# Who negates the weights: moving a per-piece negation from ScalarE to the queue that loads them

## The reference, cut to what matters

```
for l in range(2):                       # first kind
    h = rms_norm(x, norm1) * (1 + sc1) + sh1
    x = x + g1 * hybrid_mixer(h, w_in, w_out, ...)
    h = rms_norm(x, norm2) * (1 + sc2) + sh2
    x = x + g2 * conv_ffn(h, w_gate, w_val, conv_w, conv_b, w_down)
x = rms_norm(x, final_norm)
for l in range(2):                       # second kind
    h = rmsnorm(x, norm_mix_pre); proj = h @ w_in
    y_att = sliding_window_attention(...) @ w_o_att
    y_rw  = rwkv7_time_mix(...) @ w_o_rw
    x = x + rmsnorm((sigmoid(gate_a) * y_att + sigmoid(gate_b) * y_rw) @ w_out, norm_mix_post)
    x = x + rmsnorm((gelu(ua) * ub) @ w_down, norm_ffn_post)     # ua, ub = conv(rmsnorm(x) @ w_up)
    x = x + rmsnorm(sigmoid(x @ w_ple_gate) * (p @ w_ple), norm_ple)
```

## Time and profile before

| | |
|---|---|
| median of 3 runs | 4455.27 us (4441.81 to 4456.62) |
| the profiled execution, its own time | 4447.68 us |
| its span, first to last instruction | 4445.8 us |
| mean granted clock | 0.956 |
| PE busy | 3942.4 us, 89% of the span |
| VectorE, ScalarE, GpSimd busy | 2143.0, 1723.3 and 791.4 us |

### The profile page before, as it was taken

The page is one execution under the profiler, slowest core; times in us unless marked ns, Lnnn a source line. Parts: engine busy times, 40 slices in busy tenths (PEclk is TensorE's granted clock), DMA queues, the critical chain, the costliest instruction groups (busy, mean ns, idle before and its releaser), DMA issues.

```text
span 4445.8 us, 70148 instructions
## 1 busy us (share of the span) xinstructions
PE 3942.4 (89%) x29148; PEld 3156.2 (71%) x29148; DVE 2143.0 (48%) x3621; ACT 1723.3 (39%) x2512; POOL 791.4 (18%) x1108
## 2 busy tenths in 40 slices
PE   5987999898799978899999799967889999979996
PEld 4675778776588856777777588855667777758884
DVE  5674651147333146266663466125536666346603
ACT  3364222346333246344443322234534444332223
POOL 1111222211222211200001222211120000222221
PEclk9998999999899989999999899988999999989998
DMA  9844998874488853732226589954373222658894
GB/s 279 237 101 107 283 270 186 186 157 94 104 187 188 188 121 80 169 67 53 63 59 134 119 189 188 192 123 111 86 163 72 52 53 53 149 119 187 187 192 108
DMA packets 189741, 628.75 MB, mean 141 GB/s; under 512 B 22768, under 2 KB 27888, under 8 KB 189040
## 3 DMA queue, kind: packets, MB, share of 16 engines
q0 software_dynamic: 158976, 549.52, 57.2%
q1 hardware_dynamic: 24048, 65.28, 4.1%
q10 hardware_dynamic: 6400, 9.44, 0.8%
HBM read 612.63 MB, written 2.10 MB: 138 GB/s over the span
## 4 chain that ended last, share of the span: by engine, by line
PE 43%; DVE 9%; ACT 6%; DMA 3%; issue 2%; ACTq 0%; POOL 0%; DVEq 0%; SPq 0%
PE bank L214 10%; PE bank L215 10%; PE bank L216 10%; PE bank L1922 5%; PE bank L1885 1%; ACT L2078 1%; ACT at_s L1505 1%; ACT w_lo L154 1%; ACT w L2078 1%; PE bank L1983 1%; PE bank L1911 1%; PE bank L1981 1%; DVE rw_z L2340 1%; ACT gate L2078 1%; DVE at_s L1696 1%
## 5 line engine op out<-in xcount | busy, mean ns | idle before, releaser
L214 PE MATMUL bank<-h_hi,w_hi 128*128 128x512 f32 x2576 | 1067.0, 414 | 90.1 <-DMA w_lo<-in_b_wq 33.3
L215 PE MATMUL bank<-h_lo,w_hi 128*128 128x512 f32 x2576 | 1025.2, 398 | 0.0
L216 PE MATMUL bank<-h_hi,w_lo 128*128 128x512 f32 x2576 | 1023.9, 397 | 0.0
L154 ACT ACTIVATE w_lo<-w_hi 128x1024 fp32r<-128x1024 f32 (+2 forms) x552 | 556.0, 1011 | 1175.0 <-DMA w_hi<-in_a_wgv 326.2
L214 PEld LDWEIGHTS bank<-h_hi,w_hi 128*128 128x128 f32 x2576 | 489.3, 190 | 240.8 <-issue 118.0
L215 PEld LDWEIGHTS bank<-h_lo,w_hi 128*128 128x128 f32 x2576 | 489.2, 190 | 118.1 <-issue 10.8
L216 PEld LDWEIGHTS bank<-h_hi,w_lo 128*128 128x128 f32 x2576 | 487.9, 189 | 119.4
L2078 ACT ACTIVATE gate<-bank 128x512 f32<-128x512 f32 x80 | 47.8, 597 | 274.6 <-PE bank L1922 274.6
L1365 DVE TENSOR_SCALAR fa_conv<-fa_a_in,par_a 128x512 f32<-128x512 f32 x44 | 21.6, 492 | 242.2 <-ACT fa_a_in L1312 242.0
L214 PE MATMUL bank<-fa_y_hi,w_hi 128*128 128x512 f32 x352 | 137.3, 390 | 1.2 <-DMA w_lo<-in_a_wd 1.2
L214 PE MATMUL bank<-fb_y_hi,w_hi 128*128 128x512 f32 x352 | 137.1, 389 | 0.1
(11 more groups left out here) (468 smaller groups left out, 7842.7 us busy)
## 6 DMA issues: line engine op xcount, KB each, us to landing
w_hi<-in_a_wgv POOLq DMA_DIRECT2D x80, 512.0 KB, 5.4
w_lo<-in_a_wgv POOLq DMA_DIRECT2D x80, 512.0 KB, 7.7
w_hi<-in_b_wup POOLq DMA_DIRECT2D x80, 512.0 KB, 5.2
w_lo<-in_b_wup POOLq DMA_DIRECT2D x80, 512.0 KB, 7.4
w_hi<-in_a_wh POOLq DMA_DIRECT2D x48, 512.0 KB, 4.7
w_lo<-in_a_wh POOLq DMA_DIRECT2D x48, 512.0 KB, 5.7
fa_ada_raw<-in_ada SPq DMA_DIRECT2D x48, 512.0 KB, 7.4
w_hi<-in_b_wrkv POOLq DMA_DIRECT2D x48, 512.0 KB, 4.3
```

The lines of the kernel that those rows point to most:

```text
L154: st.do(st.eng.activation(self.lo[:, s], self.hi[:, s].bitcast(F32), ACT.Copy, scale=-1.0), (self.neg_made, n + 1))
L214: pe.matmul(out, self.hi[:, a], hh[:, k0 + k, :], start=first and k == 0, stop=False)
L215: pe.matmul(out, self.hi[:, a], hl[:, k0 + k, :], start=False, stop=False)
L216: mm = pe.matmul(out, self.lo[:, a], hh[:, k0 + k, :], start=False, stop=last and k == ks - 1)
```

## The change

Seven edits, made together:

1. GpSimd negates (`tensor_scalar`, one SBUF input) between the load and the adding load of a piece; all of ScalarE's calls of `ws.high` and `first_pieces` are gone.
2. The one-column Ln that brings the table in becomes `act_ready`; at most edges it stands ahead of the wait for the last product instead of behind the last square.
3. At the edges out of ma, fa, mx and fb, VectorE adds square m-1 to the sum before it handles product m, not behind it.
4. The row swaps of attention are issued on SyncE's queue, each behind ScalarE's copy.
5. In RWKV the variance product, its Ln and its Exp come ahead of the pair's k projection and first exponentials; a one-column Ln stands ahead of the copy of r.
6. In RWKV's VectorE program `rt` is formed behind `at`, the bonus product is read three chain steps later or more, the end-of-chunk factors (`bbar`) are made earlier, the product r*k*r_k is written to `kp` instead of `r`.
7. Two PSUM banks change places (2 and 3), and the waits that guard them with them.

The diff, cut to what the prediction speaks of:

```diff
+    def negate(self, pool, n):
+        s = self.span(n)
+        pool.wait_ge(self.hi_in[n % self.FLAGS], self.landed(n))
+        pool.tensor_scalar(self.lo[:, s], self.hi[:, s].bitcast(F32), -1.0, None, ALU.mult).then_inc(self.neg_made, 1)
+
     def stream(self, pool):
         added = 0
         for n, piece in enumerate(self.pieces):
             while added < (n if piece[4] else n - 1):
+                self.negate(pool, added)
                 self.add_raw(pool, added)
                 added += 1
             self.load_high(pool, n)
         while added < len(self.pieces):
+            self.negate(pool, added)
             self.add_raw(pool, added)
             added += 1
-
-    def negate(self, st, upto):
...
+    def act_ready(self, st):
+        st.settle()
+        st.do(st.eng.activation(self.run.spare[:, 0:1], self.run.eps[:, 0:1], ACT.Ln))
     def act_rstd(self, st, part=0):
         run = self.run
-        st.settle()
-        st.do(st.eng.activation(run.spare[:, 0:1], run.eps[:, 0:1], ACT.Ln))
         self.wait(st.eng, "sum", part + 1)
...
# attention, SyncE and ScalarE
+            for nr in range(2 + KD):
+                b = nr % 2
+                sp.wait_ge(p_free, nr + 1)
+                for q in range(4):
+                    sp.dma_start(sw[32 * q:32 * q + 32, b, :], raw[32 * (q ^ 1):32 * (q ^ 1) + 32, b, :])\
+                        .then_inc(sw_in[b], 16)
...
-                    for q in range(4):
-                        act.dma_start(sw[32 * q:32 * q + 32, b, :], raw[32 * (q ^ 1):32 * (q ^ 1) + 32, b, :])\
-                            .then_inc(sw_in[b], 16)
...
# RWKV, PE
                 if p:
                     decays()
-                ws.project(pe, claim("k", p), hh, hl)
-                if p == 0:
-                    decays()
                 if p >= 2:
                     pe.wait_ge(ysq_made, p - 1)
                     pe.wait_ge(xt_made, 6 * p)
                     whole("var", p - 2, bones[:, :], yq[:, :], var_made)
+                ws.project(pe, claim("k", p), hh, hl)
+                if p == 0:
+                    decays()
                 ws.project(pe, claim("r", p), hh, hl)
...
# RWKV, ScalarE
                     decays(p)
+                    if p >= 2:
+                        log_var(p - 2)
+                        rstd(p - 2)
                     first_exps(p)
-                    ws.high(st, n + 2)
                     copy_out("k", p, f, n)
...
-                if p >= 2:
-                    log_var(p - 2)
                 if p:
                     act.wait_ge(tr_made, 3 * p)
                 act.wait_ge(z_free, f + 1)
                 do(e0, ks, ACT.Square, scale=col("k_k", p), signal=(sq_made, p + 1))
-                if p >= 2:
-                    rstd(p - 2)
+                do(run.spare[:, 0:1], run.eps[:, 0:1], ACT.Ln)
                 copy_out("r", p, f + 1, n + 1)
-                act.wait_ge(ssq_made, p + 1)
-                do(e0, cum, ACT.Exp, signal=(eb_made, p + 1))
-                ws.high(st, n + 3)
                 act.wait_ge(*read("ssq", p))
                 do(kn, kn, ACT.Ln, scale=2.0 ** 20)
                 do(kn, kn, ACT.Exp, scale=-0.5, bias=run.eps[:, 1:2], signal=(rn_made, p + 1))
+                do(e0, cum, ACT.Exp, signal=(eb_made, p + 1))
...
# RWKV, VectorE: the end-of-chunk factors move from behind step(6) to behind step(3)
                 step(3)
+                do(dve.tensor_copy(ec[:, b, :], e0[:, C - 1:S:C]))
+                ends = ec[:, b, :].unsqueeze(2).broadcast_to([P, NC, C])
+                do(dve.tensor_tensor(chunks(e0), chunks(a), ends, ALU.mult), (bbar_made, p + 1))
                 keep_masked(2)
...
# mix_b, ScalarE
             for m in range(KD):
-                ws.high(st, KD + m + 1)
                 if m == KD - 1:
-                    nxt.first_pieces(st, nxt.early)
+                    edge.act_ready(st)
                 act.wait_ge(*ws.done(KD + m + 1))
                 edge.act_square(st, m, banks[m % 2][:, :])
             edge.act_rstd(st)
             for k in range(KD):
                 edge.act_high(st, k, scale)
-                if k == 1:
-                    nxt.first_pieces(st, nxt.head)
...
# mix_b, VectorE
             for m in range(KD):
+                if m:
+                    edge.dve_acc(st, m - 1)
                 edge.wait(dve, "sq", m + 1)
                 st.settle()
                 st.do(dve.tensor_copy(mixed[:, m, :], banks[m % 2][:, :]), (z_made, m + 1))
-                if m:
-                    edge.dve_acc(st, m - 1)
```

More of the change, by code:

```diff
@@ L105, in __init__ @@
         self.neg_made, self.used = sc.sem("w_neg_made"), sc.sem("w_used")
-        self.pieces, self.at, self.negated = [], 0, 0
+        self.pieces, self.at = [], 0
     def append(self, src, width, flush):
@@ L423, in dve_again, with act_again_one @@
                                                   op0=ALU.mult, op1=ALU.subtract), self.sig("lo", k))
-    def act_again(self, st, scale):
+    def act_again_one(self, st, k, scale):
         run = self.run
[L428 to L432, removed]
+        self.wait(st.eng, "xn", k + 1)
+        st.settle()
+        st.do(st.eng.activation(run.hh[:, k, :], run.w[:, k % 3, :], ACT.Identity, scale=scale[:, k:k + 1]),
+              self.sig("hi", k + 1))
 class Ada:
@@ L1244, in _ @@
             for n in range(KD):
+                if n:
+                    after.dve_acc(st, n - 1)
                 dve.wait_ge(*ws.done(first_out + n + 1))
@@ L1563, in _ @@
                     sigmoid_steps(st, mixed[:, m, :], mixed[:, m, :], (ga_made, m + 1), half)
-            again.act_again(st, gain)
-            ws.high(st, 27)
-            nxt.first_pieces(st, nxt.early)
+            for k in range(KD):
+                again.act_again_one(st, k, gain)
             st.settle()
@@ L1956, in dense @@
                 pe.wait_ge(rk_made, p + 1)
-                whole("bonus", p, bones[:, :], r, bon_made)
+                whole("bonus", p, bones[:, :], kp, bon_made)
             def scores(p, j):
@@ L1992, in lower @@
                 else:
-                    pe.wait_ge(f_free, 5 * p + 5)
-                products(2, ct, xx, cx_made)
+                    pe.wait_ge(f_free, 5 * p + 4)
+                products(3, ct, xx, cx_made)
             def inverse(p, i):
@@ L2320, in _ @@
                    (at_made, p + 1))
+                dve.wait_ge(eb_made, p + 1)
+                do(dve.tensor_tensor(rt[b], r, e0, ALU.mult), (rt_made, p + 1))
                 shift(f + 2, "v", p, v, col("mu_v", p))
-                dve.wait_ge(bon_made, p + 1)
-                do(dve.tensor_tensor(bonus[:, b, :], bank("bonus", p)[:, :], v, ALU.mult), read("bonus", p))
                 def keep_masked(j):
@@ L2358, in _ @@
                 step(5)
+                do(dve.tensor_tensor(chunks(xt[b]), chunks(mabt), each_chunk(lm[:, 3, :]), ALU.mult))
                 keep_masked(4)
-                do(dve.tensor_tensor(chunks(xt[b]), chunks(mabt), each_chunk(lm[:, 3, :]), ALU.mult))
                 step(6)
                 do(dve.tensor_tensor(chunks(xt[b]), chunks(xt[b]), one, ALU.add), (xt_made, 6 * p + 1))
-                do(dve.tensor_copy(ec[:, b, :], e0[:, C - 1:S:C]))
-                ends = ec[:, b, :].unsqueeze(2).broadcast_to([P, NC, C])
-                do(dve.tensor_tensor(chunks(e0), chunks(a), ends, ALU.mult), (bbar_made, p + 1))
+                dve.wait_ge(bon_made, p + 1)
+                do(dve.tensor_tensor(bonus[:, b, :], bank("bonus", p)[:, :], v, ALU.mult), read("bonus", p))
                 step(7)
@@ L2676, in _ @@
                 sigmoid_steps(st, sig[:, m % 2, :], banks[4 + m % 2][:, :], (sig_made, m + 1), half, free=(g_free, m + 1))
+                if m == KD - 1:
+                    after.act_ready(st)
                 if m:
```

86 lines of the change are left out of this document (23 added, 63 removed).

## The result

The changed kernel takes 4376.32 us (median of 4 runs, 4374.9 to 4377.66) against 4453.85 us before (4441.81 to 4456.62): ratio 0.9831, interval 0.9813 to 0.9849. It is 75 us faster, where 183 were forecast, and lies outside the range (4225 to 4310, and 4215 to 4365 for 8 in 10). Stages are compared in the profiled execution of each kernel, one trace each.

What follows compares the result with a forecast made beforehand. PE, busy 3942.4 us, was held by waits at stage edges and for opening weights, mostly behind ScalarE's negations. Edges 73 + openings 113 + RWKV 26 + ma 4 - VectorE 33 = 183 off 4447.7: 4265 us, range 4225 to 4310 (8 in 10: 4215 to 4365).

Steps and rivals of the forecast that it cites:

- So 0.9 to 2.5 us; I take 1.2, near ScalarE's: Length of GpSimd's negation of 1024 columns, set from ScalarE's mean of 1.01 us and VectorE's scan, 2.45 for 1024.
- it is in time, with 2.5 too (10.5): Steady MLP: issue, negation and adding load, 0.55 + 1.2 + 7.4 = 9.2 us, end before PE needs the piece at 11.2.
- Rival (d): Slow negation: beyond 3.3 us the weight ring's loop sets PE's pace; 5 us long would give 4528 us; chance 6%.
- Taken at 33 us: Cost of GpSimd's 552 negations to VectorE: 0.3 us each, 1 in 5 on the path, -33 us.
- a gain of 4: Mixer ma: ScalarE's far copies no longer stand behind a negation, 4 us in all.
- Rival (b): VectorE pays: negations slow attention, RWKV and the edges, costing 106 instead of 33 us: 4338, range 4310 to 4380; 25%.
- The edges: Between stages the last square follows its product at once: 65 us of waits go, 73 with sums at full clock.
- The openings: At stage openings adding loads are issued sooner, so weight waits shrink: 101 us, 113 with the clock.
- The clock: Half clock behind PE's waits goes too: 8 x 1 us at the edges, 12 us at six openings.
- RWKV, swaps: RWKV's reordering: net 13 us per layer, 26 us, bounds -10 and 74; attention's swaps moved to SyncE: 0.
- `bbar`: RWKV's loop: PE's eight waits for it, 10.2 us, removed by making it three steps earlier.
- The variance product: RWKV, in front of k: PE waits for ScalarE's square, 0.6 us in six pairs, -4 us.

Runs made afterwards that it cites:

- E11: Changed kernel with a plain copy in place of GpSimd's negation (low products wrong, shows times only): 4307.74 us, ratio 0.9680.
- E6: Changed kernel with GpSimd negating every piece twice, one after the other: 5179.39 us in one run.
- E13: Changed kernel with GpSimd copying only the first half of each piece's columns instead of negating (low products wrong): 4277.32 us, ratio 0.9617.
- E12: Changed kernel with edits 2 and 3 undone: 4390.13 us, ratio 0.9868.
- E2: Changed kernel with edit 1 taken back, so ScalarE negates at its old places and edits 2 to 7 stay: 4455.74 us, ratio 1.0015.
- E3: Changed kernel with RWKV in its old order (edits 5 to 7 undone), GpSimd still negating: 4410.46 us, ratio 0.9911.
- E4: Changed kernel with edit 4 taken back, attention's row swaps on ScalarE's queue again: 4380.17 us, ratio 0.9838.
- E1: Kernel before with edit 1 alone, so GpSimd negates and all else is as before: 4411.68 us, ratio 0.9917.

## Why the prediction was wrong, step by step

**The step that failed** is "So 0.9 to 2.5 us; I take 1.2, near ScalarE's". The negation takes 2.83 us, above even the bound. The nearest row of another engine bounded nothing: GpSimd's own copy takes 1.07 and its own negation 2.83. By E11 the difference is worth 67 of the missing 108 us. But the length alone would hardly have moved the forecast: by its own sum 0.55 + 2.83 + 7.4 = 10.8 us still come before the 11.2. So with it failed the cover that the text gave it, "it is in time, with 2.5 too (10.5)", which set the limit at 3.3 us as if it were sharp; with 2.8 the weights of both MLPs already come late piece after piece (fa's 14 times, 14.9 us; fb's down weights 13 times, 4.9 us). Rival (d) did not come about, but its point was soft: by the loop of E6 GpSimd sets the pace from 5.6 - (7.45 - 3.12 - 2.77) = 4.0 us on, and weights are late well before. The 67 us hold also what little less VectorE is held by the copy (249 for 306 us); the runs don't part the two.

**VectorE.** Taken at 33 us; E11 and E13 together say 46. The forecast's 0.3 us a negation was too low: 306 / 552 = 0.55. One in five on the path was somewhat high: 46 of 306 is one in seven. The place where it shows is RWKV (5.5 to 9 us of each 450, and 17 us still with the copy). Of ma's 22 us, where the forecast gave a gain of 4, 17 go with the copy, although VectorE is busy nearly as long there: they are the length's, not the holding's. Rival (b) had the mechanism of the holding, and at 4338 was the nearest of all to the measured time, but by luck: it priced at 106 us what comes out near 46, and the length's 67 us are not in it. The Trainium skill's rule in SBUF — State Buffer, section "Who interferes with whom", was the right warning. This trace agrees on which are held: VectorE's one-input passes in SBUF (L2565) and those with two SBUF inputs (the pair at 2611.71), but not those with an input in PSUM (L2564, 692 ns before and after). Its "whole instruction" this trace doesn't show: the hold added 0.8 us under a negation of 2.80.

**The edges.** Right in kind and size: 91.8 - 19.3 - 1.0 = 71.5 us where 65 were forecast without the clock, 7.2 us from last product to next at mx to fb for 7. E12 gives edits 2 and 3 14 us of it.

**The openings.** 101 forecast. The five waits of 132.5 us became, with all that took their places, 19.2 + 17.3 + 14.9 + 10.1 + 7.7 + 6.0 + 5.6 = 80.8, so some 52 were had. Query, up and output weights came nearly as written (2.84 and 3.83 us for 17.06 and 14.72). In pl the gate's own wait fell by 14 of 17 us. What failed there is p's weights, which I had let lie: their load is issued at 2878.09, when PE frees the room, as before, but with landing, negation and adding load they are there at 2892.26, and the sum of the edge, which is earlier now, no longer covers that: PE waits 8.3 and 9.0 us. With the copy pl is 15 us shorter in all. Edges and openings together make 71.5 + 52 = 123 us less waiting, but PE's idle time fell by 86 only: the other 37 came back as waits within the stages.

**The clock.** 20 us were added for half clock that goes with the waits. Most was not there: a gap of 3.83 us is followed by products of 0.63 us as one of 14.72 was (behind the 2.84 us at the query weights the clock did stay whole). By the clock's records in the two traces, half clock fell from 390 to 257 us; PE's idle time in it fell from 198 to 69, its work in it only from 192 to 188. So the mean clock rose from 0.956 to 0.971 because the idle time in which it was low is gone, not the work. PE's busy time even rose by 14.8 us, for which the runs show no cause.

**RWKV, swaps.** With GpSimd's holding apart the order gives 7.6 and 10.6 us a layer (E2; 13 each forecast), and with it 25 in both (E3, by the stages). `bbar` is gone from the waits. The variance product waits for its square in six places of a layer, 2.1 us in all after and 2.4 in E2, where 4 were put down. The swaps are worth nothing that can be told (E4).

## What to carry to other kernels

Before work is moved to an engine that hasn't done it in the trace, its length is the first thing to measure, in a run of its own: 1.8 us of one instruction decided 67 us here, and a bound from another engine's rows did not hold. The helper engine did best when it was given only the pieces whose lateness the critical engine feels (the opening ones), and left out where it slows an engine that the critical one waits for: 154 of 552 negations on GpSimd gave 145 us, all 552 gave 75.

## What the hardware showed that was not expected

- GpSimd, f32 to the rounded format: a multiplication by a constant takes 2.83 us for 1024 columns and 1.65 for 512, a copy 1.07 and 0.70. Spans on GpSimd are rough, but the starts bear it out: the adding load's issue starts 3.10 us behind the negation's start (2599.93 to 2603.03) and 1.36 behind the copy's. The Trainium skill's GPSIMD Engine Reference, section "3.1 Elementwise", has about one cycle per element for such a body, an estimate of 0.83 ns at its 1.2 GHz; the copy is near that (0.72 ns a column between the two lengths), the multiplication is not (2.3 ns).
- Its negation holds a one-input pass of VectorE from 0.49 to 1.28 us when both start together, but no pass that starts 1.4 us later, though the negation runs on; summed over the kernel the holding goes mostly with the columns (306, 249, 149 and 132 us for negation, copy, half negation, half copy). What sets it for a single pass stays open.
- The first fa stage took 417.5, 422.6 and 422.0 us in kernels whose program there is the same (the changed one, E3, E4), and 431.4 and 426.5 in E1 and E12; its transfers are the fullest of the kernel, and single traces are not compared closer than that there.
